# Mixture-of-experts encoder block: the down bias added on VectorE in each expert turn instead of by gate-weighted matmuls ahead of the experts

## The reference

```python
logits = h @ router_w + router_b
top_logit, top_idx = lax.top_k(logits, 4)
gate = softmax(top_logit)
...
g = xb @ w_gate[e] + b_gate[e]
u = xb @ w_up[e] + b_up[e]
return clamped_swiglu(g, u) @ w_down[e] + b_down[e]
...
ys = ys * slot_gate[:, None]
out = zeros.at[slot_tok].add(ys)        # and h + out is returned
```

## Time and profile before

| what | us |
|---|---|
| median of three runs | 2566.9 |
| lowest and highest run | 2562.52, 2570.47 |
| the profiled execution, its own time | 2575.11 |
| span of the profiled execution | 2573.4 |
| TensorE busy | 2425.0 |
| VectorE busy | 749.6 |
| ScalarE busy | 452.7 |
| GpSimd busy | 224.3 |

### The profile page before, as it was taken

How to read it: one execution, slowest core, us unless ns; L and a number is a source line. 1 busy time by engine, 2 the same in 40 slices (tenths; PEclk the granted TensorE clock), 3 DMA queues, 4 the chain that set the end, 5 groups by cost and what they waited for, 6 DMA issues and landing times.

```text
span 2573.4 us, 36097 instructions
## 1 busy us (share of the span) xinstructions
PE 2425.0 (94%) x15012; PEld 1858.4 (72%) x15012; DVE 749.6 (29%) x2121; ACT 452.7 (18%) x1120; POOL 224.3 (9%) x251
## 2 busy tenths in 40 slices
PE   7998999999999774799999999999999999999996
PEld 3554767777777561777888788788787878787875
DVE  4555433543444255111122122122121212121211
ACT  2333332332333130101111111111111111111110
POOL 0000000000000005011121111121100000000000
PEclk9999898998999755899999999999999999999998
DMA  3000300000000222976777788788889888888873
GB/s 144 24 2 21 125 17 1 17 17 17 17 17 9 66 93 82 386 256 225 264 271 279 264 290 292 277 292 298 321 305 326 306 325 305 326 304 325 304 267 83
DMA packets 199046, 486.41 MB, mean 189 GB/s; under 512 B 15137, under 2 KB 17313, under 8 KB 198417
## 3 DMA queue, kind: packets, MB, share of 16 engines
q1 hardware_dynamic: 176864, 442.85, 46.5%
q0 software_dynamic: 16320, 38.27, 6.4%
q10 hardware_dynamic: 5696, 2.95, 0.4%
HBM read 452.51 MB, written 38.21 MB: 191 GB/s over the span
## 4 chain that ended last, share of the span: by engine, by line
PE 59%; DMA 1%; POOL 0%; issue 0%; POOLq 0%; ACT 0%; ACTq 0%
PE gu_bank L1677 37%; PE ya_bank L1691 17%; PE yb_bank L1704 2%; PE xa_bank L1647 1%; PE xb_bank L1655 0%; DMA x_rows<-ffn_rows,tab 0%; DMA tab_b<-slot_table 0%; POOL x_rows L1445 0%; POOL sums L1488 0%; ACT y_rows L1562 0%; POOLq L1468 0%; POOL tab_b L1452 0%; ACTq L1580 0%; POOLq L1448 0%; POOLq L1452 0%
## 5 line engine op out<-in xcount | busy, mean ns | idle before, releaser
L1677 PEld LDWEIGHTS gu_bank<-xT,ring 128*128 128x128 f32 x8192 | 965.1, 191 | 15.5 <-issue 15.5
L1677 PE MATMUL gu_bank<-xT,ring 128*128 128x128 f32 (+10 forms) x8192 | 968.5, 281 | 0.7 <-issue 0.7
L1691 PE MATMUL ya_bank<-ring,hidden 128*128 128x512 f32 x1024 | 446.2, 594 | 0.0
L1605 DVE TENSOR_SCALAR g_in<-gu_bank,bias_cur 128x128 f32<-128x128 f32 (+10 forms) x256 | 91.9, 359 | 1192.2 <-PE gu_bank L1677 1192.2
L1691 PEld LDWEIGHTS ya_bank<-ring,hidden 128*128 128x128 f32 x1024 | 192.0, 190 | 230.0 <-issue 225.5
L1556 ACT ACTIVATE sig<-g_in 128x128 f32<-128x128 f32 (+10 forms) x256 | 81.3, 317 | 875.8 <-DVE g_in L1605 875.8
L484 PE MATMUL proj_bank<-w_in_sb,normT 128*128 128x512 f32 (+3 forms) x432 | 149.8, 501 | 9.8 <-DVE w_in_sb L369 8.9
L867 PE MATMUL score_bank<-mla_kT,mla_qT 96*128 96x512 f32 x256 | 140.9, 678 | 0.0
L1488 POOL DMA_INDIRECT sums<-y_rows,tab x32 | 51.7, 1616 | 963.1 <-ACT y_rows L1562 963.1
L484 PEld LDWEIGHTS proj_bank<-w_in_sb,normT 128*128 128x128 f32 (+1 forms) x432 | 70.9, 182 | 78.4 <-issue 65.6
L907 PE MATMUL mla_bank<-mla_v,probsT 128*128 128x64 f32 x1024 | 121.4, 272 | 0.0
(11 more groups left out here) (240 smaller groups left out, 1863.4 us busy)
## 6 DMA issues: line engine op xcount, KB each, us to landing
ring<-in_w_gate SPq DMA_DIRECT2D x64, 2048.0 KB, 12.3
ring<-in_w_up SPq DMA_DIRECT2D x64, 2048.0 KB, 10.6
ring<-in_w_down SPq DMA_DIRECT2D x64, 2048.0 KB, 14.2
w_in_sb<-in_w_in SPq DMA_DIRECT2D x8, 592.0 KB, 8.8
xt<-in_x SPq DMA_DIRECT2D x8, 512.0 KB, 3.9
resid<-in_x SPq DMA_DIRECT2D x8, 512.0 KB, 3.6
w_out_sb<-in_w_out SPq DMA_DIRECT2D x1, 4096.0 KB, 16.9
residual<-resid SPq DMA_DIRECT2D x8, 512.0 KB, 2.6
```

Source lines behind the costliest of these rows:

```text
L1605: v.tensor_scalar(g_in[:, f % 2, 0:width], gu_bank[:, f % 2, 0:width], bias_cur[:, f:f + 1], LIMIT, ALU.add, ALU.min).then_inc(g_ready, 1)
L1677: last = nc.tensor.matmul(gu_bank[:, f % 2, i * 256:i * 256 + width], w[:, k, c * P:(c + 1) * P], xT[:, k, 0:width], start=(k == 0), stop= ...
L1691: last = nc.tensor.matmul(ya_bank[:, h, :], hidden[:, k, 0:P], w[:, k % 4, h * 512:(h + 1) * 512], start=(k == 0), stop=(k == FC - 1))
```

## The change

In `route` the gate table `dense`, its transposes, copies, the bias matmuls and the additions to `ht` are removed, with the load of `b_down`. The residual tiles are stored to `sums` as they were read. In `experts` SyncE loads the expert's row of `b_down`, repeated over the 128 partitions, into one of two buffers `b_row`, after the fourth weight chunk of the turn, and in wide turns its column parts for the rows above 128 into `b_more`. VectorE adds it to the down product on the way out of PSUM (`bias_rows`), and ScalarE then multiplies `y_rows` with the gates in place. TensorE's wait for a free down bank is now on VectorE's addition, and the wait for the written sums is on VectorE instead of ScalarE. The same is done in the code for the overflow blocks.

```diff
@@ route: consts, SyncE, ScalarE, VectorE, TensorE @@
-            (block_no[:], io["block_no"]), (token_no[:], io["token_no"]), (b_down[:], io["b_down"]),
+            (block_no[:], io["block_no"]), (token_no[:], io["token_no"]),
...
                 for t in range(TILES):
-                    sp.wait_ge(sums_ready, t + 1)
                     sp.dma_start(io["acc"][t * P:(t + 1) * P, :], ht[:, t, :]).then_inc(sums_out, 16)
...
-                for half in range(2):
-                    act.wait_ge(dense_T, half + 1)
-                    nc.scalar.copy(denseT[:, 4 * half:4 * half + 4, :].rearrange("e t q -> e (t q)"), dense_bank[:])\
-                        .then_inc(denseT_out, 1)
...
-                for k in range(TOPK):
-                    last = v.tensor_tensor(picked[:, k], chosen[:, k], spread(gates[:, :, k], E), ALU.mult)
-                link(last)
-                v.tensor_tensor(dense[:], picked[:, 0], picked[:, 1], ALU.add)
-                link(v.tensor_tensor(picked[:, 2], picked[:, 2], picked[:, 3], ALU.add))
-                v.tensor_tensor(dense[:], dense[:], picked[:, 2], ALU.add).then_inc(dense_ready, 1)
...
-                for t in range(TILES):
-                    for half in range(2):
-                        dve.wait_ge(down_bias, 2 * t + half + 1)
-                        last = v.tensor_tensor(ht[:, t, half * 512:(half + 1) * 512], ht[:, t, half * 512:(half + 1) * 512],
-                                               xT_bank[:, half, :], ALU.add)
...
-                    for half in range(2):
-                        nc.tensor.matmul(xT_bank[:, half, :], denseT[:, t, :], b_down[:, half * 512:(half + 1) * 512],
-                                         start=True, stop=True).then_inc(down_bias, 1)
@@ experts: SyncE @@
+                def load_bias(b, at, e):
+                    if at >= 2:
+                        sp.wait_ge(biased, 2 * at - 2)
+                        if wides(at - 1):
+                            sp.wait_ge(biased_b, wides(at - 1))
+                    sp.dma_start(b_row[:, at % 2, :], io["b_down"][bass.ds(e, 1), :].rearrange("one d -> (one d)")
+                                 .partition_broadcast(P)).then_inc(b_here[at % 2], 16)
+                    if wide(at):
+                        n = parts(WIDTHS[at])
+                        q, c = P // n, D // n
+                        for j in range(n):
+                            sp.dma_start(b_more[j * q:(j + 1) * q, at % 2, 0:c],
+                                         io["b_down"][bass.ds(e, 1), j * c:(j + 1) * c].rearrange("one d -> (one d)")
+                                         .partition_broadcast(q)).then_inc(b_here[at % 2], 16)
...
                         load(at, c, e)
+                        if c == 3:
+                            load_bias(at, at, e)
@@ experts: ScalarE @@
                 def results(b, at, i):
-                    act.wait_ge(ya_done, b + 1)
                     for h in range(2):
-                        nc.scalar.activation(y_rows[:, h * 512:(h + 1) * 512], ya_bank[:, h, :], ACT.Copy,
+                        act.wait_ge(biased, b * 2 + (h + 1))
+                        nc.scalar.activation(y_rows[:, h * 512:(h + 1) * 512], y_rows[:, h * 512:(h + 1) * 512], ACT.Copy,
...
-                    if at:
-                        act.wait_ge(added, 16 * at)
-                        if wides(at):
-                            act.wait_ge(added_b, 16 * wides(at))
                     results(at, at, at % 2)
@@ experts: VectorE @@
+                def bias_rows(b, at, loads, more):
+                    dve.wait_ge(ya_done, b + 1)
+                    i = at % 2 if at < TURNS else 0
+                    dve.wait_ge(b_here[i], more * 16 + 16 * loads)
+                    if at:
+                        dve.wait_ge(added, b * 16)
+                    for h in range(2):
+                        c = slice(h * 512, (h + 1) * 512)
+                        v.tensor_tensor(y_rows[:, c], ya_bank[:, h, :], b_row[:, i, c], ALU.add).then_inc(biased, 1)
+                    if wide(at):
+                        n = D // parts(WIDTHS[at])
+                        dve.wait_ge(yb_done, wides(at) + 1)
+                        if wides(at):
+                            dve.wait_ge(added_b, 16 * wides(at))
+                        v.tensor_tensor(y_more[:, 0:n], yb_bank[:, 0:n], b_more[:, i, 0:n], ALU.add).then_inc(biased_b, 1)
...
                     turn(at, WIDTHS[at], e)
+                    loads[at % 2] += 1 + (parts(WIDTHS[at]) if wide(at) else 0)
+                    bias_rows(at, at, loads[at % 2], 0)
@@ experts: TensorE @@
                     if at:
-                        pe.wait_ge(y_out, b * 2)
+                        pe.wait_ge(biased, b * 2)
...
-                            pe.wait_ge(yb_out, wides(at))
+                            pe.wait_ge(biased_b, wides(at))
```

More of the change, by code:

```diff
@@ L1234, in _ @@
                 v.scalar_tensor_tensor(keep["left_row"][:], block_no[:], float(LEFT_W), left_row[:], ALU.mult, ALU.add)
-                for t in range(TILES):
-                    for half in range(2):
-                        dve.wait_ge(down_bias, 2 * t + half + 1)
-                        last = v.tensor_tensor(ht[:, t, half * 512:(half + 1) * 512], ht[:, t, half * 512:(half + 1) * 512],
-                                               xT_bank[:, half, :], ALU.add)
-                        if half == 0:
-                            link(last)
-                    last.then_inc(sums_ready, 1)
             @block.tensor
@@ L1283, in _ @@
                     .then_inc(ranked, 1)
-                pe.wait_ge(dense_ready, 1)
-                for half in range(2):
-                    if half:
-                        pe.wait_ge(denseT_out, 1)
-                    for t in range(4):
-                        last = nc.tensor.transpose(dense_bank[:, t * P:(t + 1) * P], dense[:, 4 * half + t, :], ident[:])
-                    last.then_inc(dense_T, 1)
-                for t in range(TILES):
-                    if t % 4 == 0:
-                        pe.wait_ge(denseT_out, t // 4 + 1)
-                    if t:
-                        pe.wait_ge(sums_ready, t)
-                    for half in range(2):
-                        nc.tensor.matmul(xT_bank[:, half, :], denseT[:, t, :], b_down[:, half * 512:(half + 1) * 512],
-                                         start=True, stop=True).then_inc(down_bias, 1)
 def wide(at):
@@ L1344, in experts @@
         y_rows = m.sb("y_rows", [P, D])
+        b_row = m.sb("b_row", [P, 2, D])
+        b_more = m.sb("b_more", [P, 2, 512])
         y_more = m.sb("y_more", [P, 512])
@@ L1379, in experts @@
         yb_out = m.sem("yb_out")
+        b_here = [m.sem(f"b_here{i}") for i in range(2)]
+        biased = m.sem("biased_e")
+        biased_b = m.sem("biased_b")
         added = m.sem("added")
@@ L1426, in _ @@
                         with sp.If(b < left):
-                            sp.wait_ge(ya_done, b + TURNS)
+                            sp.wait_ge(biased, b * 2 + 2 * TURNS)
                             for c in range(CHUNKS):
                                 load(TURNS, c, e)
+                            sp.dma_start(b_row[:, 0, :], io["b_down"][bass.ds(e, 1), :].rearrange("one d -> (one d)")
+                                         .partition_broadcast(P)).then_inc(b_here[0], 16)
                         sp.nop()
@@ L1565, in results @@
                         n = D // parts(WIDTHS[at])
[L1566 to L1567 removed]
+                        act.wait_ge(biased_b, wides(at) + 1)
+                        nc.scalar.activation(y_more[:, 0:n], y_more[:, 0:n], ACT.Copy,
                                              scale=tab_b[:, i, 1:2].bitcast(F32)).then_inc(yb_out, 1)
@@ L1618, in turn @@
                                                    g_sig[:, s % 2, 0:width], ALU.max, ALU.mult).then_inc(hidden_ready, 1)
+                def bias_rows(b, at, loads, more):
[13 more added lines that the diff above has]
+                        v.tensor_tensor(y_more[:, 0:n], yb_bank[:, 0:n], b_more[:, i, 0:n], ALU.add).then_inc(biased_b, 1)
                 v.memset(hidden[:], 0.0).then_inc(hidden_zero, 1)
                 dve.wait_ge(hidden_zero, 1)
+                loads = [0, 0]
                 for at in range(TURNS):
@@ L1634, in _ @@
                             turn(b + TURNS, LEFT_W, e)
+                            bias_rows(b + TURNS, TURNS, loads[0] + 1, b)
                         dve.nop()
```

12 lines of the change are left out of this document (removed).

## The result

| | before | changed |
|---|---|---|
| first comparison, median of 4 runs each | 2566.2 us | 2525.1 us (2522.6 to 2540.1) |
| ratio, 95% interval | | 0.985 [0.982, 0.988] |
| profiled execution (span) | 2575.11 (2573.4) us | 2527.49 (2525.6) us |
| all runs of this study, mean | 2560.7 us (100 runs) | 2533.8 us (18 runs) |

The change is faster, and by more than forecast: 41 us in the first comparison, 27 us over all runs, against 15 us.

What follows compares the result with a forecast made beforehand. The prediction took TensorE, busy 94% of the span, and what ends the routing block as bounds. Terms -15.1 - 0.86 + 0.8 = -15.2 us from the 2566.9 us median gave 2551.7 us, range 2543 to 2563 us.

Steps and rivals of the forecast that it cites:

- the end of the block: End of the routing block: without the bias work its last arrival moves from 1023.4 to 1008.3 us, -15.1 us.
- ScalarE's start: Ahead of the router's first square: one DMA issue less on ScalarE moves the whole routing chain, -0.86 us.
- the tail: After the last down product: VectorE adds before ScalarE's second half, so the end comes 0.8 us later.
- VectorE between turns: Between expert turns: additions wait for the down product, 2.0 us in all, covered by at least 1.5 us; cost nothing.
- the bias rows on SyncE's queue: In each turn: 512 KB more behind the fourth weight chunk, 1.4 us of transfer within 5.2 us idle; cost nothing.
- the gather's margin: Gather of the next turn's rows: thinnest margin 2.0 us, in turn 13; delayed some 0.4 us there; cost nothing.
- their slow issues: Routing block: three of 32 scatter issues took 1.9 to 2.4 us; they may vanish (-3.4 us) or double (+3.4 us).
- Turn 0's start: First turn's cold start at clock 0.50, 41.41 us: no change taken, bounds -3 and +3 us.
- All four rivals: More than forecast (0.08), late gather (0.13), slower by long broadcasts (0.04), and block end held by scatters, folded into late gather.
- the first: Rival for the routing block's end: scatters at their median and a short drain, 2545.9 us; chance 0.08.
- the second: Forecast step on ScalarE's constants: one load less moves the whole routing chain from the first square on, -0.86 us.
- The runs before spread by 4 us to each side: Whole kernel before: the run-to-run spread taken as a bound among the forecast's unknowns, 4 us each way.

Runs made afterwards that it cites:

- the load's -11.8 to -15.2 us: Kernel before with b_down's load moved from ScalarE's to SyncE's queue: mean 2548.8 us against 2564.0 us (-15.2), or -11.8 us against all 41 runs of the kernel before.
- after_third: Changed kernel again, unaltered, 4 runs in a later comparison: 2544.5 us, ratio 0.990 to the kernel before; its trace 2546.7 us.
- the table's differences: Load on ScalarE against none there: 2564.0 and 2548.8 us with bias matmuls in routing, 2547.6 and 2532.7 us with additions in the turns.
- after_order: Changed kernel with seven late constants loaded on SyncE's queue, w_router issued first on ScalarE's, and 48 filler matmuls before the bias-row wait: 2549.0 us, ratio 0.994.
- before_warm: Kernel before with 18 extra matmuls on TensorE behind the bias transposes, ahead of the router loop: 2552.2 us, ratio 0.997.
- before_look2: Kernel before, unaltered, one of three further traced executions: 2556.1 us, router part 71.4 us.
- after_warm2: Changed kernel with 18 extra matmuls behind the bias transposes and 68 more behind the seam, before turn 0's transposes: 2529.6 us, ratio 0.987.

## Why the prediction was wrong

**Right, to a few tenths**: the end of the block, -15.1 forecast and -15.2 measured from last scatter to seam, with GpSimd's drain last and still 2664 ns; ScalarE's start, -0.86 and -0.95 us; the tail, +0.8 us forecast and +0.6 to +1.4 us in four pairs of traces; VectorE between turns, the bias rows on SyncE's queue, the gather's margin, all costed at nothing, with no wait of TensorE in any turn behind the first. The scatters neither lost nor doubled their slow issues (974/978/2402 ns; 43.5 and 43.6 us from first to last). Turn 0's start stayed as it was. All four rivals fell: the first named the scatters and the drain, the others did not happen. So the forecast differs from the result by a thing that none of them held.

**The step that failed** is the second: "The routing chain (square, root, normed, transposes, logits, slots, scatters) starts there, so all of it moves: -0.86 us". It took the chain as rigid. The tiles in it ran at a clock of 0.50 in the trace of before, and starting them 0.9 us earlier let the clock rise to 1.00 behind their first 16 transposes: 17 us in a trace, and some 11 to 14 us on average (the load's -11.8 to -15.2 us less its 0.86 us), since the kernel before is not slow there in every execution. I had read the clock in the rows of turn 0 and put bounds on it there alone; I never read it for the stages ahead of the seam, where the chain of waits starts too late to name TensorE. A stretch of 43 us with TensorE 95% busy at 0.50 was in the trace to be seen.

**The second miss** is the bound: "The runs before spread by 4 us to each side". That came from 3 runs. One hundred span 40 us. The traces show two draws: the router's, and attention's, whose 616.7 to 635.7 us in all the traces become 585 to 588 us once the clock's deficit (one minus the granted clock, summed over the stretch) is taken off. The base was too high with it: 2566.9 us lay in the upper cluster; the mean is 2560.7 us. In the first profiled pair attention gave the change 19 us that are not its own, and the projections took 4 back; in after_third attention was again as long as before (634.5 us).

In sum over all runs: -26.9 us, of which the forecast's terms are -15.2 and the router's clock some -11 to -14; together -26 to -30 us, within the error. Projections and attention together average 883.7 us in the traces of either kind of kernel, so no share of theirs is seen. Part of the table's differences may still be theirs: its four traces have 635.7, 630.7, 621.1 and 620.9 us of attention. What attention's draw hangs on stayed open: no run altered it on purpose. Open too is why a difference of under a microsecond weights the router's: the runs show that it does, not by what.

The Trainium skill, "TensorE: Matmul & The Clock Gate", section "HAM oscillation", tells that idle gaps of TensorE bring its clock down and that each restart is paid. The traces agree for a gap of 2.99 us (after_order, then 3.46 us in place of 1.87), while one of 2.26 us did not bring it down (before_warm). The length of a restart is not fixed in them: in before_look2 TensorE was busy for all of 36.00 us at 0.50 and the clock did not come back, while turn 0's gate and up brought it back within 8 us. So a gap of under a microsecond more or less can be worth 17 us. What sets the two apart is not shown.

## What to carry to other kernels

Read the granted clock of every stage before pricing a change, above all of stages that the chain of waits leaves out: where TensorE is busy at 0.50, a change of under 1 us upstream can be worth as much as the stage would save at 1.00, here 17 us. Such a stage has two lengths, so price both, give each a chance, and take the spread of the runs from many of them. To tell a real gain from a draw, compare stage by stage at equal clock, and vary the suspected part by itself in both kernels.

## What the runs showed of the hardware

- The same eight router tiles take 5.0 or 2.7 us each. Where the loop starts at 0.50, the clock rises 2.9 to 3.6 us behind the start of its first transposes or not in the whole loop. Six of seven traces with 7.26 to 7.70 us of idle ahead of them were slow, none of six with 6.79 to 6.88 us.
- A clock that is up can be lost in a short wait: 2.99 us was enough in after_order, and 2.10 us with 0.72 us close behind it in after_warm2. It need not be: 2.26, 0.33 and 0.81 us close together left it up in before_warm.
- A broadcast of one 4 KB row to 128 partitions took 1.25 us of the DMA engines' time, no more than its bytes by the weights' rate (1.4 us).
- GpSimd's drain behind the scatters took 2664 ns both with VectorE and TensorE at work beside it and with the other four engines idle.
